# Expert down weights in six transfers of several rows per partition instead of 22 of one

## What is computed

```python
N_EXPERTS, EC_K, D_MODEL, D_FF_2 = 16, 2, 1024, 2816

def expert_choice_ffn(h, w_router, w_gate, w_up, w_down):
    B, S, D = h.shape                          # 1, 256, 1024
    cap = EC_K * S // N_EXPERTS                # 32 tokens for each expert
    aff = jax.nn.softmax((h @ w_router).astype(jnp.float32), axis=-1)
    g, idx = lax.top_k(aff.transpose(0, 2, 1), cap)
    ...
    def run_expert(args):
        wg, wu, wd, ie, ge = args              # [1024, 2816], [1024, 2816], [2816, 1024]
        xe = h[b_rows, ie]                     # the expert's 32 tokens
        he = jax.nn.silu(xe @ wg) * (xe @ wu)  # [32, 2816]
        return (he @ wd) * ge[..., None].astype(h.dtype)

    ye = lax.map(run_expert, (w_gate, w_up, w_down, idx, g))
    return jnp.zeros_like(h).at[b_idx, idx].add(ye)
```

## Time and profile before

| | |
|---|---|
| median of 3 runs | 2462.79 us |
| the three runs | 2459.95, 2462.79, 2467.64 us |
| span of the profiled execution | 2461.6 us |
| PE busy | 1919.6 us, 78% |
| PEld busy | 1032.6 us, 42% |
| DVE, ACT, POOL busy | 486.5 us, 315.3 us, 39.2 us |
| moved by DMA | 694.22 MB, mean 282 GB/s |
| median time from issue to landing, w_down in 512 KB | 12.7 us |

### The profile page before, as it was taken

How to read it: one execution, slowest core, us unless ns; L and a number is a source line. 1 busy time by engine, 2 the same in 40 slices (tenths; PEclk the granted TensorE clock), 3 DMA queues, 4 the chain that set the end, 5 groups by cost and what they waited for, 6 DMA issues and landing times.

```text
span 2461.6 us, 28842 instructions
## 1 busy us (share of the span) xinstructions
PE 1919.6 (78%) x11352; PEld 1032.6 (42%) x11352; DVE 486.5 (20%) x1107; ACT 315.3 (13%) x733; POOL 39.2 (2%) x41
## 2 busy tenths in 40 slices
PE   8898999999999998987776666566656666666666
PEld 7774887488658855644221211112111111111121
DVE  2434332125233312152101010001010100110011
ACT  1313111022122100131100000000000000000001
POOL 0010000001010000000000000000000000000000
PEclk9999999999999999998777787877788877887677
DMA  6541543442235334317999999999999999999997
GB/s 236 152 60 46 188 138 137 155 145 81 66 121 186 134 129 144 137 70 280 410 397 422 421 418 418 422 421 418 418 423 421 414 418 424 421 418 418 424 420 310
DMA packets 171899, 694.22 MB, mean 282 GB/s; under 512 B 15407, under 2 KB 61295, under 8 KB 138928
## 3 DMA queue, kind: packets, MB, share of 16 engines
q1 hardware_dynamic: 169248, 684.36, 69.9%
q0 software_dynamic: 2576, 8.85, 1.9%
HBM read 688.96 MB, written 4.19 MB: 282 GB/s over the span
## 4 chain that ended last, share of the span: by engine, by line
PE 48%; DMA 33%; SPq 9%; DVE 4%; issue 3%; DVEq 1%; ACT 1%; ACTq 0%
DMA arena<-in_w_up 28%; PE bank L534 20%; PE bank L555 9%; SPq L391 5%; PE bank L943 5%; DMA arena<-in_w_down 4%; SPq L387 3%; PE bank L541 2%; PE bank L958 2%; PE bank L672 1%; DVE arena L1582 1%; PE bank L681 1%; PE bank L742 1%; PE bank L965 1%; PE bank L592 0%
## 5 line engine op out<-in xcount | busy, mean ns | idle before, releaser
L943 PE MATMUL bank<-arena 128*32 128x512 f32 (+1 forms) x3072 | 481.8, 782 | 307.2 <-DMA arena<-in_w_up 266.0
L534 PE MATMUL bank<-arena 128*128 128x256 f32 (+1 forms) x2720 | 501.4, 346 | 8.8 <-ACT arena L980 3.4
L534 PEld LDWEIGHTS bank<-arena 128*128 128x128 f32 x2720 | 445.0, 193 | 63.4 <-issue 4.8
L943 PEld LDWEIGHTS bank<-arena 128*32 128x32 f32 x3072 | 111.3, 139 | 674.8 <-DMA arena<-in_w_up 361.3
L958 PE MATMUL bank<-arena 128*32 128x256 f32 x2816 | 250.2, 473 | 91.6 <-DMA arena<-in_w_down 91.3
L555 PE MATMUL bank<-arena 128*128 128x512 f32 x544 | 235.5, 593 | 1.2 <-ACT arena L1162 1.2
L958 PEld LDWEIGHTS bank<-arena 128*32 128x32 f32 x2816 | 84.5, 125 | 251.4 <-issue 221.3
L1582 DVE TENSOR_TENSOR arena<-arena,bank 64x256 f32<-64x256 f32 x96 | 38.6, 402 | 751.7 <-ACT arena L1181 750.1
L555 PEld LDWEIGHTS bank<-arena 128*128 128x128 f32 x544 | 102.7, 190 | 127.6 <-issue 126.1
L1181 ACT ACTIVATE arena<-bank 64x512 f32<-64x512 f32 (+1 forms) x48 | 23.2, 550 | 834.0 <-PE bank L943 834.0
L1461 DVE SCALAR_TENSOR_TENSOR arena<-bank,arena 128x254 f32<-128x254 f32 (+1 forms) x176 | 76.8, 477 | 194.6 <-ACT arena L1121 191.3
(11 more groups left out here) (255 smaller groups left out, 1196.2 us busy)
## 6 DMA issues: line engine op xcount, KB each, us to landing
arena<-in_w_down SPq DMA_DIRECT2D x364, 512.0 KB, 12.7
arena<-in_w_gate SPq DMA_DIRECT2D x128, 1408.0 KB, 19.5
arena<-in_w_up SPq DMA_DIRECT2D x128, 1408.0 KB, 22.5
arena<-in_w_up SPq DMA_DIRECT2D x44, 1024.0 KB, 7.5
arena<-in_w_in SPq DMA_DIRECT2D x40, 1024.0 KB, 7.3
arena<-in_w_down SPq DMA_DIRECT2D x16, 1024.0 KB, 5.7
arena<-in_w_out SPq DMA_DIRECT2D x12, 1024.0 KB, 7.2
bias_rows<-arena POOLq DMA_DIRECT2D x1, 3072.0 KB, 45.4
```

The source lines that it names most:

```text
L534: last = mm(ps[bank][:, j * S + lo:j * S + lo + n], w[:, k, c:c + P], xT[:, k, lo:lo + n], start=(k == 0), stop=(k == KT - 1))
L943: last = mm(ps[b][32 * q:32 * q + 32, 0:n], expert_x[:, k, :], gate_up_ring[:, s_, q // 2, c:c + n], start=(k == 0), stop=(k == KT - 1))
```

## The change

The down weights of an expert come in CHUNKS = 6 transfers, three for each half, of 512, 512 and 384 rows of the weights: partition p of a transfer gets four (or three) rows that follow each other in memory, p R to p R + R - 1 of the piece, with R = 4 or 3. In SBUF they stand side by side in the partition: a buffer for each of the three pieces, together as large as the ring of eleven. `down_free` counts pieces, so a transfer of the second half waits until PE has used all rows of the same piece of the first half, and PE waits for one landing for each piece. The products of a piece are the same in number and size; row r of every partition stands where transfer k stood. So that `hidden_t` fits, block r must be the columns r, r + R, r + 2R, ... of the piece: DVE's products read both inputs with a step of R elements and write as before.

```diff
-GU_RING, D_RING = 4, 11
+GU_RING = 4
 ...
+CHUNKS = 2 * len(PIECES)
 ...
-        down_ring = down_region.take(D_RING, D)
+        down_ring = [down_region.take(n // P, D) for _, n in PIECES]
 ...
-            def down(e, k):
-                sp.dma_start(down_ring[:, k % D_RING, :], a["w_down_2"][0, bass.ds(e, 1), k * P:(k + 1) * P, :].rearrange("o p n -> (o p) n")
-                             ).then_inc(sem(f"d_in{k % D_RING}"), 16)
+            def down(e, j):
+                b = j % len(PIECES)
+                c0, n = PIECES[b]
+                lo = j // len(PIECES) * HALF + c0
+                sp.dma_start(down_ring[b].rearrange("p r n -> p (r n)"), a["w_down_2"][0, bass.ds(e, 1), lo:lo + n, :].rearrange("o (p r) n -> (o p) (r n)", p=P)
+                             ).then_inc(sem(f"d_in{b}"), 16)
 ...
-            def stream_down(e, ks):
-                for k in ks:
-                    sp.wait_ge(sem("down_free"), e * FT + k + 1)
-                    down(e, k)
+            def stream_down(e, js):
+                for j in js:
+                    sp.wait_ge(sem("down_free"), e * CHUNKS + j + 1)
+                    down(e, j)
 ...
-                for k in range(FT):
-                    pe.wait_ge(sem("expert_hidden_copied"), e * 3 + (k // 4 + 1 if k < HT else 3))
-                    pe.wait_ge(sem(f"d_in{k % D_RING}"), e * (FT // D_RING * 16) + 16 * (k // D_RING + 1))
-                    for q in range(4):
-                        last = mm(ps[5][32 * q:32 * q + 32, 0:256], hidden_t[:, k % HT, 32 * (k // HT):32 * (k // HT) + 32], down_ring[:, k % D_RING, 256 * q:256 * q + 256],
-                                  start=(k == 0), stop=(k == FT - 1))
+                for j in range(CHUNKS):
+                    half, b = j // len(PIECES), j % len(PIECES)
+                    R = PIECES[b][1] // P
+                    if half == 0:
+                        pe.wait_ge(sem("expert_hidden_copied"), e * 3 + b + 1)
+                    pe.wait_ge(sem(f"d_in{b}"), e * 32 + 16 * (half + 1))
+                    for r in range(R):
+                        for q in range(4):
+                            last = mm(ps[5][32 * q:32 * q + 32, 0:256], hidden_t[:, 4 * b + r, 32 * half:32 * half + 32], down_ring[b][:, r, 256 * q:256 * q + 256],
+                                      start=(j == 0 and r == 0), stop=(j == CHUNKS - 1 and r == R - 1))
                     last.then_inc(sem("down_free"), 1)
 ...
-                        blocks = lambda y: y.rearrange("p (m n) -> p m n", n=P)[:, odd::2, :][:, 0:m, :]
+                        blocks = lambda y: y.rearrange("p (c r) -> p r c", c=P)[:, odd::2, :]
                         last = w.tensor_mul(hidden[64 * odd:64 * odd + 64, 2 * b:2 * b + m, :], blocks(expert_gate[0:64, c0:c0 + n]), blocks(ps[b][64:P, 0:n]))
```

More of the change, by code:

```diff
@@ L382, in _ @@
             sp.sem_inc(sem("gate_up_free"), GU_RING)
-            sp.sem_inc(sem("down_free"), D_RING)
+            sp.sem_inc(sem("down_free"), len(PIECES))
             def gate_up(e, k):
@@ L399, in _ @@
             gate_up(0, 3)
-            for k in range(D_RING):
-                down(0, k)
+            for j in range(len(PIECES)):
+                down(0, j)
             sp.wait_ge(sem("rows_used"), (DEPTH + 1) * ROW_UNITS + 2)
@@ L409, in stream_gate_up @@
                     gate_up(e, k)
-            def stream_down(e, ks):
-                for k in ks:
-                    sp.wait_ge(sem("down_free"), e * FT + k + 1)
-                    down(e, k)
+            def stream_down(e, js):
+                for j in js:
+                    sp.wait_ge(sem("down_free"), e * CHUNKS + j + 1)
+                    down(e, j)
             stream_gate_up(0, range(GU_RING, KT))
             stream_gate_up(1, range(0, 2))
-            stream_down(0, range(D_RING, FT))
+            stream_down(0, range(len(PIECES), CHUNKS))
             stream_gate_up(1, range(2, KT))
-            stream_down(1, range(FT))
+            stream_down(1, range(CHUNKS))
             with sp.Fori(2, NE) as e:
                 stream_gate_up(e, range(KT))
-                stream_down(e, range(FT))
+                stream_down(e, range(CHUNKS))
             for t in range(T):
@@ L1185, in _ @@
                     last.then_inc(sem("expert_hidden_copied"), 1)
-                act.wait_ge(sem("down_free"), e * FT + FT + D_RING)
+                act.wait_ge(sem("down_free"), e * CHUNKS + CHUNKS + len(PIECES))
                 for q in range(2):
@@ L1580, in expert @@
                         m = 2 if odd == 0 or b < 2 else 1
-                        blocks = lambda y: y.rearrange("p (m n) -> p m n", n=P)[:, odd::2, :][:, 0:m, :]
+                        blocks = lambda y: y.rearrange("p (c r) -> p r c", c=P)[:, odd::2, :]
                         last = w.tensor_mul(hidden[64 * odd:64 * odd + 64, 2 * b:2 * b + m, :], blocks(expert_gate[0:64, c0:c0 + n]), blocks(ps[b][64:P, 0:n]))
                     last.then_inc(sem("expert_hidden"), 1)
-                v.wait_ge(sem("down_free"), e * FT + FT + D_RING)
+                v.wait_ge(sem("down_free"), e * CHUNKS + CHUNKS + len(PIECES))
                 for q in (2, 3):
```

## The result

The changed kernel takes **2476.15 us** (median of 6 runs, 2470.72 to 2482.31); the kernel before, run beside it, 2464.18 (2459.95 to 2468.58). The ratio is 1.0047, 95% interval 1.0033 to 1.0062: slower by 8 to 15 us, where 2453 with a range up to 2467 was forecast. The sign holds in both. The size is 10 to 12 us by the two ratios, and 7.5 by the medians of the later runs (2470.93 against 2463.41).

A forecast was written before the change was run, and what follows sets the result against it. The DMA queue was taken to bound experts 1 to 15. Packets -17.7, refill stalls with DVE +5, expert 0 +1.3 and the end +1.7 make -9.7 us from 2462.8: 2453 us, range 2444 to 2467.

The forecast's parts named there:

- Part 1: Down weights of experts 1 to 15: larger packets move faster, saving 1.18 us an expert, 17.7 us in all.
- The spare: Refill in ten experts: fourth piece issued early enough to keep the queue from running dry, by 0.4 to 1.0 us.
- part 2: Refill of the fourth down piece: queue dry at T + 12.9 (T: PE's last gate/up step starts), costing 0.9 us.
- Part 3: DVE's strided products: 1.0 us more an expert delays the refill; stalls taken as 5 us in all.
- The chance of 0.2: Rival on DVE's products: they are dearer still than the forecast took; chance 0.2.
- Part 4: Three rows, not one, after the last landing: 1.3 us later in expert 0, 1.7 us at the end.
- The rival on the slower side: Expert stage: queue runs dry in nearly every expert waiting for the first piece; 2475 us, chance 0.08.
- the restart: DMA queue at the refill: 0.95 us from issue to first packet.

The follow-up runs named there:

- e4: The kernel before, with single rows, but SP waits until a group of 4, 4 or 3 rows is free: 2472.55 us, ratio 1.0036.
- e9: The changed kernel with only the gate half of the next expert's first step ahead of the second half of down: 2450.35 us, ratio 0.9943.
- e1: The changed kernel with the next expert's first gate and up step ahead of the second half of down on SP: 2449.12 us, ratio 0.9944.
- e3: The changed kernel with DVE reading runs of 128 as before, row order not undone, so only its time counts: 2464.24 us, ratio 1.0004.
- e6: e1 with DVE reading runs of 128 as in e3, row order not undone: 2447.70 us, ratio 0.9939.
- e5: e1 with its six transfers made of 4096 B packets again and DVE reading runs of 128: 2464.85 us, ratio 1.0011.
- e7: The changed kernel run again, unchanged, for a second profile: 2470.93 us, ratio 1.0040.
- e8: The changed kernel with the first piece of each half in two transfers of two rows (8192 B packets): 2465.45 us, ratio 1.0015.

## Why the prediction was wrong, step by step

**Part 1, packets: right.** By the packets of the traces (medians), 4096 B took 164 ns and 11264 B 425 in before, where 160 and 423.8 were worked out from the beat, and 2048 B 86 (84.7 by the line); in after 16384 B took 613 ns and 12288 B 460, where 612 and 461.5 were worked out.
The first of these, the uneven end, stood in the trace of before. The earlier trace rows begin at 2444.65, the last byte, and I took that for the end of all. The windows just ahead of it, at the end of the last down row:

```profile
2442.00:2443.00 1.00, 0.80 (x11) 0.23 (x8) 0.00 (x0) 0.00 (x0) 0.00 (x0) 0.50 1.03 410
2443.00:2443.50 0.50, 0.50 (x8) 0.00 (x0) 0.00 (x0) 0.00 (x0) 0.00 (x0) 0.50 0.90 360
2443.50:2444.00 0.50, 0.31 (x8) 0.09 (x8) 0.00 (x0) 0.00 (x0) 0.00 (x0) 0.50 0.31 123
2444.00:2444.65 0.65, 0.65 (x8) 0.14 (x8) 0.00 (x0) 0.00 (x0) 0.00 (x0) 0.50 0.05 19
```

The rate falls from about 2443.2, 1.4 us ahead of the last byte. By the packets of the same trace, 16 are under way at 2443.0, five at 2443.8 and one from 2444.0 to 2444.4: in before too the engines end up to 1.4 us apart. The spare of "0.4 to 1.0 us" that part 2 gave to ten experts was thus none: nearly all were late from the start, with 17.9 to 23.6 us of stall instead of 5. e4 shows this without the change's other parts (8 us), e9 and e1 show that lead is the cure.

**Part 3, DVE: right in size, wrong in its price.** The products end 3.31 us after the first starts, not 2.51: 0.8 us, where 1.0 was taken. A 64x256 product that reads every fourth element takes 600 ns instead of 424, 0.69 ns more for each element; one that reads every third takes 493, only 0.27 more; why the step of three is cheaper than the step of four no run shows. The 1.0 us was my estimate, taken between 0 and the 1.4 us that another 1.02 ns an element would add. The chance of 0.2 was for products dearer still; no run shows such a cost, only the 0.8 us. By the forecast these reads cost 4 us. With the refills already late, each 0.1 us of them was paid in most of the experts: 0.8 x 12 or so, and e3 measures some 10. e6 shows that the price is zero with cover.

**Part 4, coarse finish: wrong at both places.** Expert 0 cost +0.4 instead of +1.3, and the end came 1.8 us *sooner* instead of 1.7 later. I had the last rows at the slower clock, 0.50 granted in the earlier trace rows, and the placing left as it was. (The prediction's figures in GHz stand for the granted clocks 0.50 and 1.00; the traces show the clock only as a share of full speed.) After the change PE waits for whole pieces, and the clock granted in the last rows and the placing, at the end of expert 0 and of the kernel, is 1.00. The three rows behind the last landing end 1.5 us after it, where one row ended 1.2 after it: 0.3 us more, not 1.7. The eight placing matmuls take 3.70 us instead of 6.21 in expert 0 and 6.67 at the end, where before had granted clocks of 0.59 and 0.55. In expert 0 this hides a refill that was 2.5 us late (the last down landing is at T + 30.1 instead of 27.6), where I had -0.6 + 0.2. It is no chance of one profile: in the eight profiles of kernels with whole pieces (e5 with its 4096 B packets too) 127 of 128 placings take 3.70 us, in the three of kernels with single rows 17 of 48, the others 5.2 to 6.7; the granted clock is 1.00 in every placing of 3.70 us and 0.55 to 0.70 in the others. I had also written that the queue is empty from 1217.31 to 1228.06 in expert 0; windows of before have more than 400 GB/s there until about 1228.5, and next to nothing (11 GB/s) from 1230 to 1233.2. The gap is at the start of expert 1, and a later start still makes it longer. Timeline of after in expert 0, timeline and window of its end, then of before's end:

```profile
1227.03 1.50 PE L966 MATMUL bank<-arena 128*32 128x256 f32 x24 [0.27 <-DMA arena<-in_w_down]
1229.52 3.70 PE L973 MATMUL bank<-arena 128*128 128x512 f32 x8 [0.99 <-DVE arena L1594]
...
2461.43 3.70 PE L973 MATMUL bank<-arena 128*128 128x512 f32 x8 [0.99 <-DVE arena L1594]
...
2461.00:2465.00 4.00, 3.57 (x8) 1.44 (x8) 1.66 (x3) 0.50 (x2) 0.00 (x0) 1.00 0.00 0
...
2447.24 6.67 PE L965 MATMUL bank<-arena 128*128 128x512 f32 x8 [0.98 <-DVE arena L1586]
...
2446.00:2452.00 6.00, 5.02 (x10) 2.18 (x7) 1.79 (x4) 0.75 (x2) 0.00 (x0) 0.50 0.00 0
```

**The rival on the slower side had the mechanism:** dry in nearly every expert, 12 to 15 us for each further us of delay, and among its causes "a restart slower than 0.95 us". Its sum passed +7.4 at 2.3 us of delay; what came was 0.8 us of DVE and a limit 1.6 us earlier, 2.4 together, beyond the forecast of part 2 without DVE. That its 2475 lies so near the measured 2476 is partly luck: its stall of 24.7 us was right (23.6), but its 3.3 + 1.7 for expert 0 and the end were 0.4 - 1.8. I gave it 0.08, since I had taken the restart as measured and asked only of PE and DVE whether they might be later. The spare of ten experts, 0.4 to 1.0 us, hung on one reading, and the four windows above would have turned it into a lack of 0.4 to 1.0.

With the sizes measured: -17.7 (packets) + 23.6 or 17.9 (stalls) + 0.4 (expert 0) - 1.8 (end) = +4.5 or -1.2 us for the two profiled executions from expert 0 on, and +4.8 and -1.0 are in the traces. The medians are 12.0 and 7.5 us apart, so 7 to 8.5 us of the loss against before are not accounted for by these stages. Part may be that the stalls vary and e7's profile is of its fastest run; part may lie ahead of the experts, where the same code ends at other times in each profile and the profile of before has the earliest of all, though its whole lies near the median. How it is shared out, over many runs, no profile shows, and it stays open. The comparison that doesn't hang on one profile is e1 and e9 against the changed kernel, 21 to 27 us by medians.

## What to carry to other kernels

Larger packets paid here on a queue that is always full (17.2 us, e5 beside e6), but they come with larger pieces, and the wait for a whole piece uses up the lead of the refill; look for the lead first. With pieces of 2 MB, an issue 2.8 us ahead of the last byte (T + 10.1) lost less than 0.2 us, one 2.0 us ahead (T + 10.95) 0.3 to 1.3, and in e9 one expert lost 0.7 at 3.7. If your lead is shorter than 3 us, put a transfer that needs no wait ahead of the refill, as e1 and e9 do. Take as "dry" the moment at which the rate begins to fall in windows of 1 us, not the last byte, which came 1.4 us later at the end of before and 1.6 in expert 6 of the changed kernel. Where an engine's delay (here DVE's 0.8 us an expert) reached the queue by way of a late refill, it cost in most rounds, some 10 us in all (e3); with cover no cost could be told (e6, ratio 0.9939 against e1's 0.9944).

## What was not expected of the hardware

- The 16 engines do not end a transfer together: from the fall of the rate to the last byte it is some 1.5 us (1697.5 to about 1699 in expert 6; 2443.2 to 2444.65 in the kernel before), and the first 16384 B packets after a gap take 1.35 us on average instead of 0.61.
- A tenths row of 9 hides this: the DMA share of the experts is 0.99 with the stalls and 1.01 without; GB/s (417 against 425) shows it.
- The line of 9.3 ns and 0.0368 ns per byte, made from 4096 and 11264 B (164 and 425 ns in the packets of before), held at 16384 B (612 ns, 613 measured), at 12288 B (461.5, 460) and at 8192 B: 309 to 311 ns at the steady places of e8, against 311.
- How PE waits goes with the clock that it is granted for what follows: behind down weights in whole pieces the placing has a granted clock of 1.00 (3.70 us) in 127 of 128 experts, behind rows with a short wait each in 17 of 48.
- The runs of e3 and e7 lie far apart (16 and 13 us), those of the covered e6 and e9 close together (5.7 and 3.6 us). It is no rule: e1, covered, has 9.5 us, and e4, late, 5.1.
